# One encoder layer on one core: the mixers move from five whole-sequence phases into groups of two tiles that stand between the expert slots

## The reference

```python
u = rmsnorm(h); proj = u @ w_in            # 1024 x (768 + 2576 + 1536)
A: attention over 2 chunks of 64, 8 heads on 2 key heads, ALiBi, sinks
B: Mamba-2 scan: causal conv of 4 taps, 16 heads, state 128, gate SiLU(z)
C: attention over 9 chunks, 8 heads, a learned bias per relative distance
h += concat(rmsnorm(A), rmsnorm(B), rmsnorm(C)) @ w_out     # 2048 x 1024
q = rmsnorm(h) @ w_query                   # 8 heads x 2 halves x 128
per head: top 16 of 128 scores for each half, top 16 of the 256 sums -> 16 expert rows
h += sum_e gelu(u . peer_u[e]) * gate[e] * peer_v[e]        # 8 x 16 = 128 experts a token
h += sigmoid(rmsnorm(h) @ w_gate) * (p @ w_proj)
```

## Time and profile before

| | us |
|---|---|
| median of 3 timed runs | 4203.33 (4196.61 to 4206.89) |
| the profiled execution | 4196.09 |
| its span, first to last instruction | 4194.1 |
| TensorE busy in the span | 2606.0 (62%) |
| VectorE busy | 2275.8 (54%) |
| GpSimd busy | 1994.7 (48%) |
| ScalarE busy | 561.3 (13%) |
| bytes moved by DMA | 1163.07 MB, mean 277 GB/s |

### The profile page before, as it was taken

The page is one execution under the profiler, slowest core; times in us unless marked ns, Lnnn a source line. Parts: engine busy times, 40 slices in busy tenths (PEclk is TensorE's granted clock), DMA queues, the critical chain, the costliest instruction groups (busy, mean ns, idle before and its releaser), DMA issues.

```text
span 4194.1 us, 32340 instructions
## 1 busy us (share of the span) xinstructions
PE 2606.0 (62%) x10286; PEld 1229.7 (29%) x10286; DVE 2275.8 (54%) x5239; ACT 561.3 (13%) x1213; POOL 1994.7 (48%) x2087
## 2 busy tenths in 40 slices
PE   8989999999786124444445554454454454443796
PEld 4645665544543111111111111111111111110232
DVE  2321223013633998676767676767676767665210
ACT  2431324011620000000000000000000000000120
POOL 0000000000311557777777777777777777776454
PEclk9889999899898667777676666767767667665898
DMA  2015230200223889999999999999999999999886
GB/s 80 1 42 37 37 23 21 62 20 21 81 105 123 318 296 385 409 409 410 409 409 409 409 409 407 408 406 405 406 408 405 400 406 407 400 408 406 322 326 248
DMA packets 344076, 1163.07 MB, mean 277 GB/s; under 512 B 49256, under 2 KB 58608, under 8 KB 342896
## 3 DMA queue, kind: packets, MB, share of 16 engines
q0 software_dynamic: 294912, 1073.87, 65.2%
q1 hardware_dynamic: 49008, 87.26, 8.1%
HBM read 1145.72 MB, written 15.27 MB: 277 GB/s over the span
## 4 chain that ended last, share of the span: by engine, by line
DMA 28%; POOL 16%; DVE 12%; issue 7%; PE 6%; ACT 0%; SPq 0%; POOLq 0%; PEldq 0%; DVEq 0%; ACTq 0%
DMA peer_u_ring<-peer_u,peer_idx_u 24%; POOL peer_v_ring L1274 8%; POOL peer_u_ring L1263 8%; DVE peer_u_ring L1487 6%; DMA peer_v_ring<-peer_v,peer_idx_v 3%; PE ps L1672 3%; PE ps L1641 2%; DVE peer_hot L1444 1%; DVE peer_hot L1441 1%; DVE peer_halves L1445 1%; PE ps L1682 1%; DVE peer_best_i L1415 0%; DVE peer_cand L1416 0%; PE ps L1662 0%; DVE peer_best_i L1418 0%
## 5 line engine op out<-in xcount | busy, mean ns | idle before, releaser
L1641 PE MATMUL ps<-peer_v_ring,peer_spread 128*32 128x512 f32 x4096 | 854.1, 978 | 1232.5 <-DMA peer_v_ring<-peer_v,peer_idx_v 1232.5
L1487 DVE CUSTOM_DVE_ANT_0 peer_u_ring<-peer_u_ring,ps 128x1024 f32<-128x1024 f32 x1024 | 1239.6, 1220 | 680.3 <-DMA peer_u_ring<-peer_u,peer_idx_u 668.9
L1263 POOL DMA_INDIRECT peer_u_ring<-peer_u,peer_idx_u x1024 | 971.5, 949 | 521.6 <-DVE peer_dots L1487 273.4
L1274 POOL DMA_INDIRECT peer_v_ring<-peer_v,peer_idx_v x1024 | 965.8, 943 | 391.2 <-issue 301.8
L1641 PEld LDWEIGHTS ps<-peer_v_ring,peer_spread 128*32 128x32 f32 x4096 | 166.8, 149 | 1640.1 <-issue 1640.0
L786 POOL MEMSET b_xbc<- 128x36 f32 x1 | 0.1, 134 | 722.2 <-POOLq L94 722.2
L1598 PE MATMUL ps<-wq,peer_uT 128*128 128x256 f32 x1024 | 325.5, 463 | 0.7 <-ACT peer_uT L1298 0.7
L1598 PEld LDWEIGHTS ps<-wq,peer_uT 128*128 128x128 f32 x1024 | 226.5, 239 | 198.2 <-issue 167.2
L1312 ACT ACTIVATE peer_q<-ps 128x256 f32<-128x256 f32 x64 | 24.5, 383 | 1397.7 <-PE ps L1598 1397.7
L505 PE MATMUL ps<-c_w,wq 128*128 128x256 f32 (+1 forms) x512 | 170.4, 496 | 14.3 <-DMA c_w<-w_in 14.3
L874 PE MATMUL ps<-wq,bp_w 128*128 128x512 f32 x384 | 165.0, 592 | 0.0
(11 more groups left out here) (258 smaller groups left out, 3094.1 us busy)
## 6 DMA issues: line engine op xcount, KB each, us to landing
peer_u_ring<-peer_u,peer_idx_u POOLq DMA_INDIRECT x1024, 18.1
peer_v_ring<-peer_v,peer_idx_v POOLq DMA_INDIRECT x1024, 18.0
bp_w<-w_in SPq DMA_DIRECT2D x4, 2048.0 KB, 7.6
wq<-b_cs_rows SPq DMA_DIRECT2D x8, 1024.0 KB, 4.7
wq<-peer_w_query SPq DMA_DIRECT2D x2, 4096.0 KB, 18.6
c_w<-w_in SPq DMA_DIRECT2D x24, 256.0 KB, 4.9
h<-x SPq DMA_DIRECT2D x8, 512.0 KB, 7.1
bout_w<-w_out SPq DMA_DIRECT2D x4, 1024.0 KB, 8.5
```

Of the source, the lines that this page charges most:

```text
L1263: nc.gpsimd.indirect_dma_start(u_ring[:, n % RU, :], None, io["peer_u"][0], bass.IndirectOffsetOnAxis(ap=idx_u[:, t % 2, h * TOPK + s:h * ...
L1274: nc.gpsimd.indirect_dma_start(v_ring[:, n % RV, :], None, io["peer_v"][0], bass.IndirectOffsetOnAxis(ap=idx_v[:, t % 2, token:token + 1], ...
L1487: nc.vector.tensor_tensor_reduce(out=row, in0=row, in1=un_ps, scale=1.0, scalar=0.0, op0=ALU.mult, op1=ALU.add, accum_out=dots[:, t % 2, h ...
L1641: last = nc.tensor.matmul(acc_ps[32 * j:32 * j + 32, half * 512:(half + 1) * 512], centres[:, at:at + 32], v_ring[:, n % RV, half * 512:(h ...
```

## The change

Everything becomes one program (`whole_program`), a list of steps that each of the five engines walks in the same order. `front_steps(g)` is all of the work of the mixers, the output projection and the queries for tiles 2g and 2g + 1. The front of group 0 stands ahead of slot 0. Those of groups 1, 2 and 3 are spread over slots 0 to 197, 198 to 453 and 454 to 709, by the numbers in `PACE`. The scores of each query go to DRAM and come back when their retrieval is due. The embeddings of tiles 0 to 6 are spread from slot 752 on. Each step knows by a plan (`plan_banks`) which PSUM bank it takes and whose copy frees it: the slots hold 4 of the 8 banks, the fronts have `W` (two banks), `X` and `Y`.

The weights don't stay: each front streams 35 blocks of 1 MB (1 KB rows) through a ring of three, four times in all. The rings of the gathers shrink. The root of each norm is made by Ln and Exp on ScalarE, and the state's decay goes from GpSimd to VectorE. C's bias table is made once, masked, kept in DRAM, and read again by each group.

```diff
-            normalise_input(nc, core, uT, io["x"][0], io["mix_norm"][0], io["peer_sub_keys"][0])
-            mixer_a(nc, core, uT, y, spare, io)
-            mixer_c(nc, core, uT, y, spare, io)
-            mixer_b(nc, core, uT, z, stream, io)
-        peer_and_gate(nc, core, stream, out[0], io)
...
-    RU, RV = 8, 12
+GT = 2
+GROUPS = TILES // GT
+RW, UNIT = 3, 256
+RU, RV, Q = 6, 8, 4
...
+    return (norm + first + a_in + blend(a_steps(g), c_project_steps(g)) + [("c_bias", g, 0), ("c_bias", g, 1)]
+            + blend(c_steps(g), x_steps(g)) + b_steps(g) + o_steps(g)
+            + [(st, t) for t in tiles for st in ("n2", "n2_t")] + query_steps(g))
...
+PACE = dict(norm=2.4, a_p=3.7, a_turn=1.5, a_s=0.9, a_t=1.2, a_v=0.9, c_p=3.7, c_t=0.7, c_s=1.2, c_u=1.2, c_v=0.9, x=3.7, dt=1.8,
+            cs=0.4, z=3.7, b_turn=3.5, b_off=1.8, b_diag=2.0, b_state=1.8, y_t=2.0, o=7.4, n2_t=2.4, q=3.7, q_t=0.7, q_s=0.7)
...
+FRONT_ENDS = [256 * g - 58 for g in range(1, GROUPS)]
+GATE_AT = [752, 804, 856, 908, 960, 1012, 1060]
...
+    for g, end in zip(range(1, GROUPS), FRONT_ENDS):
+        steps = front_steps(g)
+        cost = np.cumsum([PACE.get(st[0], 0.2) for st in steps])
+        for st, c in zip(steps, cost):
+            todo.setdefault(done + int((end - done) * c / (cost[-1] + 0.01)), []).append(st)
+        done = end
...
+    for n in range(SLOTS):
+        out += slot_steps(n) + todo.get(n, [])
...
+    def load_block(u):
+        if u >= RW:
+            end = next(step for step, blocks in k.block_end.items() if u - RW in blocks)
+            b = k.bank[end]
+            sp.wait_ge(k.filled[b.place], b.n + 1)
+        sp.dma_start(k.wr[:, u % RW], k.blocks[u % UNITS]).then_inc(k.w_in[u % RW], 16)
...
+        if step == ("sub", 3):
+            spread_c_bias()
+            keep_sub_keys()
...
+    def inverse_root(mean, width):
+
+        chain.link(act_fn(mean, mean, ACT.Ln, scale=1.0 / width, bias=k.eps[:, 0:1]))
+        return act_fn(mean, mean, ACT.Exp, scale=-0.5)
...
+    def head_roots(o, heads):
+        act.wait_ge(k.sq_sum, o + 1)
+        inverse_root(k.hm[:, o % 4, 0:heads], HD).then_inc(k.rs_full, 1)
```

More of the change, by code:

```diff
@@ L713, with blend, c_items @@
[L713 to L719 removed]
+        self.eng.wait_ge(self.sem, self.n)
+def blend(*lists):
+    at = [((i + 0.5) / len(steps), n, i) for n, steps in enumerate(lists) for i in range(len(steps))]
+    return [lists[n][i] for _, n, i in sorted(at)]
+def c_items(g, half):
+    return [(half * 4 + i, g * GT + lt) for i in range(4) for lt in range(GT)]
@@ new lines, in c_project_steps, with c_steps @@
+def c_project_steps(g):
+    units = [(t, kind, j) for kind in "kvq" for j in range(2) for t in range(g * GT, g * GT + GT)]
+    out, turn = [], []
+    for t, kind, j in units:
+        if len(turn) > 1:
+            out.append(("c_t", *turn.pop(0)))
+        out.append(("c_p", t, kind, j))
+        if kind != "v":
+            out.append(("c_n", t, kind, j))
+            turn.append((t, kind, j))
+    return out + [("c_t", *u) for u in turn]
+def c_steps(g):
+    out = []
+    for half in range(2):
+        items, units = c_items(g, half), c_units(g, half)
+        out += [("c_s", g, half, 0), ("c_s", g, half, 1)]
+        ahead = 2
+        for u, parts in enumerate(units):
+            out.append(("c_u", g, half, u))
+            for n, k in parts:
+                if k == items[n][1] and ahead < len(items):
+                    out.append(("c_s", g, half, ahead))
+                    ahead += 1
+            if u:
+                out.append(("c_v", g, half, u - 1))
+        out += [("c_v", g, half, len(units) - 1), ("c_o", g, half)]
+    return out + [(st, "c", g * GT + lt) for lt in range(GT) for st in ("y_n", "y_t")]
@@ L791, in _ @@
[L791 removed]
+            gpsimd_program(nc, pool, k, io)
         @block.scalar
         def _(act):
[L795 to L804 removed]
```

3036 lines of the change are left out of this document (1580 added, 1456 removed).

## The result

The changed kernel took **4330.9 us** (median of four runs, 4321.7 to 4334.1) beside 4203.5 of the kernel before (four runs, 4196.6 to 4206.9): a ratio of **1.030 [1.028, 1.032]**. The forecast was 4060, faster, within 3870 to 4330. Its direction was wrong.

A forecast was written before the change was run, and what follows sets the result against it. The prediction took TensorE to bound the mixers while DMA idles, then VectorE, then mostly DMA the slots. Head 630, group 1's slots 650, groups 2 and 3 1690, the rest 828 and 256 sum to 4054; it said 4060, range 3870 to 4330.

The forecast's parts named there:

- Scan, norms and A's projection together I put at 36 us: Groups 2 and 3: stalls beyond DMA's 809 us, giving 845 us each.
- A block is not what is late here: Groups 2 and 3: a 1 MB block takes about 6 us, and one is wanted every 7 slots.
- Region by region, each at the slower of its engines: Group 1's slots: front regions priced by their slower engine, with VectorE's slots at 1.65 and its waits, in sum 650 us.
- The 809 us of DMA: Groups 2 and 3, per 256 slots: 669 us of slots and 140 us of the front's bytes.
- sum of stages: Whole kernel: head 630, group 1's slots 650, groups 2 and 3 1690, then 828 and 256: 4054 us.
- Forecast 650: Slots 0 to 197 beside group 1's front: 650 us, from below VectorE's 556.
- The 76: Head, output projection: two norms' waits of 11, 8 x 7.2 and the late blocks, put at 76 us.
- two sets of four buffers in turn: Last 140 slots, v alone: 8 buffers alternate as two sets, 12.5 us for 8, giving 224 us.
- Lockstep: Rival, chance 0.25: front and slot steps take turns across engines; slower, 4660 us fully, 4360 half way.
- The ideal overlap: Rival, chance 0.18: stalls vanish in the gather rings, total 3840 to 3950 us.
- GpSimd was not held: Denies the rival, chance 0.07, that VectorE's two-input products stop GpSimd's gather issues: no change, 4170 to 4215 us.
- The drain before each table load: ScalarE: the skill's about 1.38 us per load would make the sum about 4200; the forecast went without it.

The follow-up runs named there:

- e1: The changed kernel loading only an eighth of each weight block in groups 1 to 3: 4106.8 us, ratio 0.976 to the kernel before.
- e5: The changed kernel with the output projection in two passes, holding one weight block at a time: 4249.4 us, ratio 1.011 to the kernel before.
- e2: The changed kernel with an Identity in place of the norms' logarithm, leaving the root out: 4217.6 us, ratio 1.003 to the kernel before.
- e8: The changed kernel with a u ring of 4 buffers instead of 6: 4432.5 us, ratio 1.055 to the kernel before.
- e7: The changed kernel with an eighth of the blocks in groups 1 to 3 and no logarithm: 3968.4 us, ratio 0.944 to the kernel before.
- e17: The changed kernel with output halves, bias table from DRAM, late norms in groups 1 to 3, and group 1's front by slot 150: 4244.9 us, ratio 0.963.

## Why the prediction was wrong

**The step that failed** is the price of the waits that a front brings into the slots: "Scan, norms and A's projection together I put at 36 us" for each of groups 2 and 3, with nothing for the other regions and "A block is not what is late here", and in group 1 "Region by region, each at the slower of its engines". The runs show 96 and 89 us in groups 2 and 3 for the 36, and 82 more than forecast in group 1. The 809 us of DMA for groups 2 and 3 held. No term of the sum of stages has the wrong sign, but each came out longer, and 278 us of such errors are more than the 140 between the forecast and no change.

- *Bytes: priced rightly.* Windows over the regions of group 2's front, cut where TensorE begins the next region: the norm with A's projection, the rest of A with C's projection, C with the conv, scan with z, the output projection, the last norms, the queries.

```profile
1394.00:1467.00 73.00, 43.59 (x201) 26.05 (x201) 34.16 (x84) 34.17 (x58) 30.55 (x32) 0.74 0.87 319
1467.00:1634.00 167.00, 107.09 (x584) 64.70 (x580) 106.49 (x287) 64.42 (x135) 95.89 (x102) 0.82 0.98 370
1634.00:1869.00 235.00, 171.56 (x929) 112.70 (x929) 160.60 (x399) 66.28 (x157) 132.17 (x140) 0.78 0.98 369
1869.00:1994.00 125.00, 86.39 (x383) 54.86 (x382) 83.29 (x166) 29.45 (x55) 60.09 (x63) 0.77 0.87 313
1994.00:2123.00 129.00, 82.69 (x401) 56.31 (x399) 64.88 (x156) 8.07 (x15) 67.18 (x72) 0.80 0.95 357
2123.00:2150.00 27.00, 3.69 (x22) 3.19 (x19) 7.94 (x24) 5.66 (x8) 5.61 (x6) 0.61 0.78 295
2150.00:2303.00 153.00, 114.90 (x551) 72.85 (x554) 90.48 (x217) 17.98 (x55) 92.98 (x99) 0.81 1.03 395
```

  The queries stream blocks like the others, and there gathers and blocks together move 395 GB/s; the best slices of the other regions have 396 to 406. At 400 the 325 MB of group 2 (909 x 358) are 813 us and the 321 MB of group 3 are 802, where 809 was forecast. (At the 407 of the slots alone they would be 799 and 788, and the stalls below 13 us more each.) e1 says the same: 95 and 81 us came back for bytes forecast at 86, 13 of the 95 as stalls. I had the rate for rows of 1 KB from C's weights loaded with nothing beside the earlier trace rows, and beside the gathers it was no worse.
- *Stalls in groups 2 and 3: forecast 36 us, measured 96 and 89*, the time beyond these 813 and 802. By region, time less bytes at 400 GB/s, group 2 loses 15, 12, 18, 27, 14, 7 and 2 us. Scan, norms and A's projection are 49 of it, for 36. A with C's projection, C with the conv and the output are 44 more, and these I had put at nothing, with no more reason than that DMA stays the bound "on the average". Reckoned so, group 2 has 85 us of stalls in e5 (362 GB/s in its 899 us), 75 in e2 (366 in 889) and 154 in e8, all three with the same bytes, and 83 in e1 and 47 in e7 with fewer. Late blocks, the waits for roots and the ring's depth each move it. What makes up the rest was not tried one by one.
- *Why the DMA share hides this.* A share of 0.95 looks like 45 us of idle time, and the forecast's 36 like nearly right. But busy time isn't bytes. The gathers' queue (packets, MB, share of 16 engines), in slots 198 to 453 of the kernel before (673 us), of the changed kernel (909 us) and of e8 (967 us); last the weights' queue of the changed kernel:

```profile
q0 software_dynamic: 74693, 271.99, 101.3%
```

```profile
q0 software_dynamic: 73898, 269.09, 77.6%
```

```profile
q0 software_dynamic: 73743, 268.52, 73.8%
```

```profile
q1 hardware_dynamic: 45039, 55.68, 17.3%
```

  That is 2.51, 2.62 and 2.66 us a MB for the same gathers, and 2.61 in e1, where seven eighths of the blocks' bytes are gone. In the kernel before, from 1357 to 1587 us, where VectorE sets the pace and no front is there, the same packets take 2.84 (84.4% of 230 us for 68.3 MB). So they get longer where the gathers don't follow one another closely, not by the blocks beside them. The front's own transfers took 157 us, less 8 of the kernel before in that queue: 149 for the 140 forecast.
- *Late blocks.* In the head they were priced at 5 us, four times, and TensorE waits 16.4 us for them there: right. Beside the slots they were put at nothing, because the gate's 4 MB had landed in 23.7 us; TensorE waits 45.0 us at the output projection in group 1 and 27.7 in group 2. The changed kernel's landings, in the columns of that row:

```profile
front<-w_in SPq DMA_DIRECT2D x76, 1024.0 KB, 10.4
front<-w_out SPq DMA_DIRECT2D x32, 1024.0 KB, 16.5
front<-peer_w_query SPq DMA_DIRECT2D x32, 1024.0 KB, 16.6
...
front<-ple_w_gate SPq DMA_DIRECT2D x1, 4096.0 KB, 25.4
```

  The gate is taken in rows of 4 KB, a block in rows of 1 KB, and 1 MB of these takes two thirds of the time of 4 MB of the others (that the row length does it was not tried alone, nor was a longer ring of blocks). Halves brought back 67 to 81 us (e5), most of it in the head and in group 1.
- *Group 1.* Forecast 650, measured 732, the worst single stage. Its regions, in the order above, were forecast at 57, 125, 138, 107, 68, 20 and 133 us and took 47, 145, 176, 97, 121, 24 and 123. The two that are far off, C with the conv and the output:

```profile
849.00:1025.00 176.00, 118.10 (x519) 98.44 (x518) 117.82 (x312) 54.87 (x131) 47.32 (x49) 0.71 0.64 199
...
1122.00:1243.00 121.00, 73.64 (x324) 56.37 (x324) 58.50 (x144) 7.32 (x14) 48.75 (x51) 0.79 0.80 288
```

  The output's 53 too many are the late blocks in the main: with halves it takes 85 us (e5). In C with the conv no engine is busy for more than 118 of 176 us, and neither e5, e1 nor e2 shortens it by more than 5: there the engines take turns, and "the slower of its engines" is no price for that. Which hand-overs make it up wasn't tried, and stays open. Of the whole stage the runs return 30 (halves), 50 (no logarithm), 56 (blocks), 102 (the last two). The waits for head norms were priced rightly (45; the row of the changed kernel has 40.3 in 657 to 1394), the output's weren't (VectorE's wait for it is 60.9 there). e17 shows that a front's chain takes 596 us with 150 slots in it while the DMA engines have room.
- *Head.* 657 for 630. The stall behind the table was forecast from 80 to 188 and is in the chain that ends last:

```profile
84.33 104.92 issue
189.24 5.79 PE ps L1539 x16
```

  Behind it A with C's projection took 75 us for 80, C with the conv 104 for 90, scan and z 91 for 79, the output 83 for 76, the norms 17 for 17, and the rest 98 for 100. The 76 is below its own parts: 11, 8 x 7.2 and four times 5 are 89. The 24 us that halves return here are mostly late blocks that were in the sum, so they don't explain the 27.
- *Rest.* 854 for 828 in slots 710 to 1023 at an unchanged share of 1.02. The kernel before takes 833 there, not 821; the other 21 us, for which I had 7, fit with more bytes: beside the gathers this stretch moves 18 MB where it moved 9. In the tail it is 287 for 256. Its price took two sets of four buffers in turn; TensorE waits 105.2 us for v there, 32 times. No run took the tail apart further.

**The rivals.** Lockstep (0.25) is the one that came true in its number: it was to decide from 3.50 us a slot over all 710 slots, and the slots took (732 + 909 + 893)/710 = 3.57. It was right that stalls cross the rings (e8), and that the norms' waits cost even at a DMA share of 0.95 (e2). Its full size was not reached: of the 237 us that group 2's slots take over the kernel before, 96 are stalls and the rest is the front's bytes. But these stalls are what the forecast missed. The ideal overlap, which put stalls at nothing, had 811 us a group for 909 and 893. GpSimd was not held: its median issue is 937 ns, 941 before, and the slowest 1753 for 1939. The Trainium skill (SBUF — State Buffer, Who interferes with whom), which the prediction names for it, limits this contention to GpSimd instructions that read SBUF. The drain before each table load is not in the trace (the page of the profile has 1.8 us of idle time before 104 loads), so the row was the right price.

## What to carry to other kernels

An overlap is paid in the bytes that it adds to the busy resource, and in the stalls that the added work brings into it. Here the bytes were priced within 1% and the stalls at well under half. So go through the added work region by region and ask of each at what rate the bound resource will run beside it; a region put at nothing needs a reason. Afterwards measure the bound resource by what it moves, against what it moves where nothing disturbs it: the DMA engines' share stood at 0.95 where a tenth of the time was lost. An experiment that takes bytes away and one that takes waits away, alone and together, say which to mend. What a phase hides for nothing, as the old projection hid the bias table, has to be made cheap before the phase is shortened.
